# Retention: values centred per head in place of the outputs, no mean products, the variance a head sooner, decay powers ahead of the normalization

## The reference, cut to what matters

```python
def retention_branch(q, k, v, gate, log_decay, pad):
    ...
    q = rotate(q, pos, XPOS_THETA, RET_QK_DIM) * (RET_QK_DIM ** -0.5)
    k = rotate(k, pos, XPOS_THETA, RET_QK_DIM)
    ...
    o = retention_dir(qc, kc, vc, log_decay[0], True) + flip(
        retention_dir(flip(qc), flip(kc), flip(vc), log_decay[1], False))
    ...
    mu = jnp.mean(o, axis=-1, keepdims=True)
    var = jnp.mean(jnp.square(o - mu), axis=-1, keepdims=True)
    o = (o - mu) * lax.rsqrt(var + EPS)
    o = o.reshape(B, L, RET_V).astype(gate.dtype)
    return o * jax.nn.silu(gate)
```

## Time and profile before

| what | value |
|---|---|
| median of 3 runs | 4152.93 us (4151.59 to 4163.54) |
| profiled execution, span from first to last instruction | 4148.7 us |
| profiled execution's own time around it | not shown apart; the span is 4.2 us below the median |
| TensorE busy | 3974.4 us, 96% |
| VectorE, ScalarE, GpSimd busy | 54%, 35%, 21% |
| mean granted clock of TensorE | 0.975 of 2.4 GHz |

### The profile page before, as it was taken

How to read it: one execution, slowest core, us unless ns; L and a number is a source line. 1 busy time by engine, 2 the same in 40 slices (tenths; PEclk the granted TensorE clock), 3 DMA queues, 4 the chain that set the end, 5 groups by cost and what they waited for, 6 DMA issues and landing times. The chain is left out here.

```text
span 4148.7 us, 55847 instructions
## 1 busy us (share of the span) xinstructions
PE 3974.4 (96%) x22416; PEld 3453.2 (83%) x22416; DVE 2243.2 (54%) x3931; ACT 1471.3 (35%) x2120; POOL 860.5 (21%) x777
## 2 busy tenths in 40 slices
PE   8999999999899999999999999999999999999998
PEld 7877799999684568888777886789999998999997
DVE  4333446445434344645547544347997675666664
ACT  3144345222314433522237343333333333333332
POOL 1000013111200001312101520016756553111100
PEclk9998999999998999999989999999999999999999
DMA  3101123222110112322212022236756778888873
GB/s 132 52 31 41 46 82 112 92 87 96 57 62 27 45 46 92 119 91 102 81 61 77 31 67 66 87 98 202 227 186 194 247 251 272 286 265 265 265 245 122
DMA packets 232448, 519.43 MB, mean 125 GB/s; under 512 B 36160, under 2 KB 134592, under 8 KB 231808
## 3 DMA queue, kind: packets, MB, share of 16 engines
q1 hardware_dynamic: 160752, 400.75, 29.1%
q0 software_dynamic: 18432, 67.12, 4.6%
q10 hardware_dynamic: 53008, 47.99, 3.4%
HBM read 454.66 MB, written 60.82 MB: 124 GB/s over the span
## 5 line engine op out<-in xcount | busy, mean ns | idle before, releaser
L304 PE MATMUL PSM<-UX,PARTS 128*128 128x264 f32 (+3 forms) x3392 | 1192.3, 351 | 44.5 <-DVE UX L333 26.5
L305 PE MATMUL PSM<-UX,PARTS 128*128 128x264 f32 (+3 forms) x3392 | 1173.0, 346 | 0.0
L306 PE MATMUL PSM<-UX,PARTS 128*128 128x264 f32 (+3 forms) x3392 | 1169.8, 345 | 0.0
L272 DVE TENSOR_TENSOR PARTS<-RAW,PARTS 128x1024 fp32r<-128x1024 f32 x549 | 687.0, 1257 | 614.8 <-ACT PARTS L262 565.5
L262 ACT ACTIVATE PARTS<-RAW 128x1024 fp32r<-128x1024 f32 x612 | 644.8, 1056 | 993.7 <-PE PSM L306 493.3
L304 PEld LDWEIGHTS PSM<-UX,PARTS 128*128 128x128 f32 x3392 | 652.1, 192 | 134.5 <-DVE UX L333 37.0
L305 PEld LDWEIGHTS PSM<-UX,PARTS 128*128 128x128 f32 x3392 | 651.9, 192 | 60.3 <-issue 3.1
L306 PEld LDWEIGHTS PSM<-UX,PARTS 128*128 128x128 f32 x3392 | 651.4, 192 | 59.8
L2555 PE MATMUL PSM<-AC,PARTS 128*128 128x448 f32 x1024 | 374.7, 366 | 4.1 <-DVE AC L2802 4.1
L2557 PE MATMUL PSM<-AC,PARTS 128*128 128x448 f32 x1024 | 374.0, 365 | 0.0
L2556 PE MATMUL PSM<-AC,PARTS 128*128 128x448 f32 x1024 | 373.9, 365 | 0.0
(11 more groups left out here) (378 smaller groups left out, 5754.7 us busy)
## 6 DMA issues: line engine op xcount, KB each, us to landing
RAW<-w_ff_dram SPq DMA_DIRECT2D x128, 512.0 KB
RAW<-peer_u_dram SPq DMA_DIRECT2D x128, 512.0 KB
RAW<-peer_v_dram SPq DMA_DIRECT2D x128, 512.0 KB
RAW<-w_in_dram SPq DMA_DIRECT2D x116, 512.0 KB
acts_dram<-MQ ACTq DMA_DIRECT2D x128, 224.0 KB
MQ<-acts_dram SPq DMA_DIRECT2D x128, 224.0 KB
MQ<-gates_dram SPq DMA_DIRECT2D x128, 224.0 KB
RAW<-w_mix_o_dram SPq DMA_DIRECT2D x32, 512.0 KB
```

The lines of the kernel that those rows point to most:

```text
L272: e.tensor_tensor(p[:, 1024:2048], self.raw.of(i), p[:, 0:1024].bitcast(F), SUB).then_inc(V.sem, V.tick("w", i))
L304: e.matmul(dst, wh[k], xh_[k][:, lo:hi], start=(k == 0), stop=False, skip_group_check=True)
L305: e.matmul(dst, wh[k], xl_[k][:, lo:hi], start=False, stop=False, skip_group_check=True)
L306: m = e.matmul(dst, wl[k], xh_[k][:, lo:hi], start=False, stop=(k == kk - 1), skip_group_check=True)
```

## The change

- Each pair of heads' values is centred where it lies, over the 128 channels of each head, on VectorE right behind its copy out of PSUM (`centred_dve`): a sum and a subtraction for 16 rows and for 128 rows. The fourth group's centring stands behind the first head's decays.
- The mean product, its PSUM buffer and the subtraction out of PSUM are gone. ScalarE copies the sum and squares it, both straight from PSUM.
- The gate tile and the variance product of head h - 1 (before, h - 2) stand between scores and values of head h, so the stage has 9 rounds in place of 10.
- The decay powers of heads 0 and 1 are made in the projection stage; the exponential of the rates moves to its start.
- The scaling of head h - 2 on VectorE stands between the second and third score of head h.
- TensorE begins the scores when the last rotated tile is there (before, when VectorE had ended the projection stage).

```diff
@@ in_act @@
                 rstd_act(e, ("pre", l), TT, rsX, 1.0 / D, "ss", 7)
+                all_ = MH[:, oVec + 80:oVec + 112]
+                e.activation(all_, all_, ACT.Exp).then_inc(S.sem, S.tick("lg"))
...
             for t in range(5):
                 tok(t)
+                if t in (2, 3):
+                    decays_act(e, l, t - 2)
@@ in_dve @@
             for t in range(1, 5):
                 tok(t)
+                if t < 4:
+                    centred_dve(e, l, t)
+                if t < 3:
+                    logs_dve(e, l, t - 1)
...
+        def centred_dve(e, l, t):
+
+            c = 256 * (t - 1)
+            e.wait_ge(S.sem, S.at("tok", l, t, 3))
+            for (r, j0, j1), m in zip(((16, 0, 1), (128, 1, 5)), means[t - 1]):
+                x = vR[0:r, j0:j1, c:c + 256].rearrange("p j (a n) -> p j a n", a=2)
+                y = m[0:r].rearrange("p (j a) -> p j a", a=2)
+                e.wait_ge(V.sem, V.n)
+                e.tensor_reduce(y, x, AX.X, ADD).then_inc(V.sem, V.tick())
+                e.wait_ge(V.sem, V.n)
+                e.scalar_tensor_tensor(out=x, in0=y.unsqueeze(3).to_broadcast([r, j1 - j0, 2, 128]),
+                                       scalar=-1.0 / 128, in1=x, op0=MUL, op1=ADD).then_inc(
+                                           V.sem, V.tick("centred", l, t))
@@ ret_pe @@
-            e.wait_ge(V.sem, V.at("end", ("in", l)))
-            for h in range(10):
+            e.wait_ge(V.sem, V.at("rot", l, 12))
+            for h in range(9):
...
-                if h >= 2:
-                    i = first["fill", l] + h - 2
-                    tile_pe(e, ("g", l, h - 2), i, W.both(i), us(c0, n), n)
+                if h >= 1:
+                    i = first["fill", l] + h - 1
+                    tile_pe(e, ("g", l, h - 1), i, W.both(i), us(c0, n), n)
+                    b, back = ps.take("ss", ("ret", l, h - 1))
...
+                    e.wait_ge(S.sem, S.at("dev2", l, h - 1))
+                    gemm(e, b, [con["onesm"]], [sq2[(h - 1) % 2][:, 0:n]], n).then_inc(
+                        T.sem, T.tick("var", ("ret", l, h - 1)))
...
-                    gemm(e, b, [con["onesm"]], [sq2[h % 2][:, 0:n]], n).then_inc(T.sem, T.tick("var", ("ret", l, h - 2)))
-                if 1 <= h < 9:
-                    b, back = ps.take("mean", l, h - 1)
...
-                    gemm(e, b, [con["onesm"]], [oS[h - 1][:, 0:n]], n).then_inc(T.sem, T.tick("mean", l, h - 1))
@@ ret_act @@
+            for h in range(9):
+                if h >= 1:
+                    decays_act(e, l, h + 1)
+                    W.act(e, first["fill", l] + h - 1 + 3)
...
+                    rstd_act(e, ("ret", l, h - 1), n, sq2[(h - 1) % 2], 1.0, "var")
                 if h < 8:
                     e.wait_ge(T.sem, T.at("ret", l, h, 4))
                     e.activation(fv(oS[h][:, 0:n], n), pv(ps.of("ret", l, h), n), ACT.Copy).then_inc(
                         S.sem, S.tick("o", l, h))
+                    if h >= 2:
+                        e.wait_ge(V.sem, V.at("normed", l, h - 2))
+                    e.activation(fv(sq2[h % 2][:, 0:n], n), pv(ps.of("ret", l, h), n), ACT.Square).then_inc(
+                        S.sem, S.tick("dev2", l, h))
                     ps.give(S, "ret", l, h)
@@ ret_dve @@
-                if 1 <= h < 9:
-                    o = oS[h - 1]
-                    e.wait_ge(T.sem, T.at("mean", l, h - 1))
-                    e.scalar_tensor_tensor(out=fv(o[:, 0:n], n), in0=pv(ps.of("mean", l, h - 1), n), scalar=-1.0,
-                                           in1=fv(o[:, 0:n], n), op0=MUL, op1=ADD).then_inc(V.sem, V.tick("dev", l, h - 1))
-                    ps.give(V, "mean", l, h - 1)
+            for h in range(9):
                 if h < 8:
+                    decays(h, (0, 1))
+                if h >= 2:
+                    normed(h - 2)
+                if h < 8:
+                    decays(h, (2, 3, 4))
+                    if h >= 1:
+                        logs_dve(e, l, h + 1)
+                    else:
+                        centred_dve(e, l, 4)
+                if h >= 1:
+                    W.dve(e, first["fill", l] + h - 1 + 3)
+            normed(7)
```

More of the change, by code:

```diff
@@ L424, in program @@
         sq3, rsX = [wt(i) for i in range(3)], wt(3)
+        means = [(WK[:, 3 * TT + 16 * t:3 * TT + 16 * t + 2], WK[:, 3 * TT + 16 * t + 2:3 * TT + 16 * t + 10]) for t in range(4)]
         rx, ry, ut = [wt(4 + i) for i in range(3)], [wt(7 + i) for i in range(2)], [wt(9 + i) for i in range(3)]
@@ L578, in in_dve, with logs_dve, decays_act @@
             sin(12)
+            if l == 0:
+                e.wait_ge(S.sem, S.at("lg"))
+                for i in (0, 2):
+                    ap = MH[:, oVec + 80 + 8 * i:oVec + 88 + 8 * i]
+                    e.tensor_scalar(ap, ap, -1.0, None, MUL).then_inc(V.sem, V.tick())
             for t in range(1, 5):
                 tok(t)
+                if t < 4:
+                    centred_dve(e, l, t)
+                if t < 3:
+                    logs_dve(e, l, t - 1)
             stage_end(V, ("in", l))
+        def centred_dve(e, l, t):
[10 more added lines that the diff above has]
+                                           V.sem, V.tick("centred", l, t))
+        def logs_dve(e, l, h):
+            if h < 8:
+                dt = DT[h % 2]
+                e.wait_ge(V.sem, V.n)
+                e.tensor_scalar(dt, con["rel"], lg(l, 0, h), None, MUL).then_inc(V.sem, V.tick())
+                e.wait_ge(V.sem, V.n)
+                e.scalar_tensor_tensor(out=dt, in0=con["rel"], scalar=lg(l, 1, h), in1=dt, op0=MUL,
+                                       op1=MIN).then_inc(V.sem, V.tick("logs", l, h))
+        def decays_act(e, l, h):
+            if h < 8:
+                e.wait_ge(V.sem, V.at("logs", l, h))
+                e.activation(DT[h % 2], DT[h % 2], ACT.Exp).then_inc(S.sem, S.tick("decays", l, h))
         def in_pool(e, l):
@@ L645, in ret_act @@
             after_all(e, ("in", l))
[L646 to L661, removed]
+            for h in range(9):
+                if h >= 1:
+                    decays_act(e, l, h + 1)
+                    W.act(e, first["fill", l] + h - 1 + 3)
+                    e.wait_ge(T.sem, T.at("g", l, h - 1))
+                    if h >= 3:
+                        e.wait_ge(G.sem, G.at("gated", l, h - 3))
+                    e.activation(fv(gx[(h - 1) % 2][:, 0:n], n), pv(ps.of("g", l, h - 1), n), ACT.Silu).then_inc(
+                        S.sem, S.tick("g", l, h - 1))
+                    ps.give(S, "g", l, h - 1)
+                    rstd_act(e, ("ret", l, h - 1), n, sq2[(h - 1) % 2], 1.0, "var")
                 if h < 8:
@@ new lines, in decays @@
+            def decays(h, js):
+                dt = DT[h % 2]
+                for j in js:
+                    j0, nj = JT[j]
+                    e.wait_ge(T.sem, T.at("score", l, h, j))
+                    if j == 0:
+                        e.wait_ge(S.sem, S.at("decays", l, h))
+                    i = 5 * h + j
+                    if i >= 6:
+                        e.wait_ge(T.sem, T.at("ret", l, (i - 6) // 5, (i - 6) % 5))
+                    win = dt[0:nj, c0 - j0 + 400:c0 - j0 + 400 + n]
+                    e.scalar_tensor_tensor(out=fv(sd[i % 6][0:nj, 0:n], n), in0=pv(ps.of("score", l, h, j), n, nj),
+                                           scalar=0.125, in1=fv(win, n), op0=MUL, op1=MUL).then_inc(
+                                               V.sem, V.tick("decay", l, h, j))
+                    ps.give(V, "score", l, h, j)
```

59 lines of the change are left out of this document (7 added, 52 removed).

## The result

The changed kernel takes 4084.9 us (median of 4 runs, 4078.9 to 4090.1), the kernel before beside it 4152.3. The ratio is 0.9835, 95% interval 0.9815 to 0.9855. The profiled execution of the changed kernel took 4083.3 us, its span is 4081.5. The forecast was 4085. One execution of the experiment with waits of 1.23 us ran in a slow state (5623.5 us at a granted clock of 0.65) and is left out of that ratio.

The account below looks back on a forecast made before the run. TensorE's own sequence was taken to bound the kernel. Gains of 29.4 and 32.1 us in the stages and 2.6 and 4.1 in the tails sum to 68.2, giving 4085 us; own range 4078 to 4093, asked-for range 4076 to 4103.

Parts of the forecast that it names:

- Products: Retention stages: eight mean products in each layer leave TensorE, 8 x 0.97 + 8 x 0.94 = 15.3 us, all on the path.
- Waits and clock: Both retention stages: TensorE's waits go, 8.7 us in layer 0 and 9.1 in layer 1, and 28.5 us of clock return.
- the choice that the clock comes back: Retention stages: without waits the granted clock returns, worth 28.5 us, because the stretch 194 to 225 ran at 1.00.
- the closing waits: End of each retention stage: TensorE's wait for the squares, 0.52 us in layer 0 and 0.97 in layer 1, goes.
- (a): Rival, retention stages: the clock stays low because the half-array score mix makes the dips; 38.7 us won, 4114; chance 0.09.
- (d): Rival, retention stages: the denser sequence holds the clock down; at 60% half rate 31 us slower, 4184; chance 0.02.
- No new wait: Heads of the retention stages: PSUM buffers and squares are ready in time, so TensorE gets no new wait.
- 1.5 us and more to spare: Third and fourth scores of a head: the PSUM buffers they take are free at least this long before.
- Centring: VectorE in the projection: 3.4 us a group of two heads, hidden with 2.6 us cover; cost 0.
- Tails: Last gate product to first transposed attention product: 8.9 us in layer 0, 2.6 won; 10.9 in layer 1, 4.1 won.

## Why the prediction was right

*Products.* 15.3 us forecast. Put back alone they cost 13.8 to 16.6, and 13.9 by the heads of the trace. Shown, with a price per product some 0.1 us too high.

*Waits and clock.* 17.8 us of waits and 28.5 of clock, on the choice that the clock comes back. The split has a slip: the closing waits of 0.52 and 0.97 us lie behind the stages' ends at 339.9 and 1387.0. So the 61.5 us hold 16.3 of waits and some 30 of clock, and the sum is the same. The stages came out at 130.6 and 126.0 us where 130.7 and 126.2 were worked out, at a clock of 1.00. That the clock hung on the waits and not on the products is shown from both sides: taking only the waits out of the kernel before brought 33 to 37 us for 11.3 us of idle time, and putting ten waits of 1.23 us into the changed kernel took as much away. The rivals (a) and (d) are out. What decides whether a single wait brings a dip was not found. Of the two sections of the page "TensorE: Matmul & The Clock Gate" of the Trainium skill that the prediction weighs, "A second HAM failure mode: psum-queue depth-cycling", with its short idles between groups of products, fits these runs. The long waits for transfers of the other one, "HAM oscillation — how this bites in real kernels", were not needed: in the stages of the kernel before TensorE never waits for a transfer, its longest wait is 1.4 us, and the clock fell.

*No new wait.* ScalarE's order held: no head waits for the square or the logarithm. ScalarE in the changed kernel around the end of a head's values (222.66):

```profile
220.97 0.64 ACT L354 ACTIVATE WK<-WK 128x528 f32<-128x528 f32 x1
222.77 0.61 ACT L696 ACTIVATE WK<-PSM 128x528 f32<-128x528 f32 x1 [1.15 <-PE PSM L200]
223.28 0.60 ACT L700 ACTIVATE WK<-PSM 128x528 f32<-128x528 f32 x1
```

It is free 1.15 us before the copy can start, and the square ends at 223.9, 1.6 us ahead of the fourth score, which comes 2.9 us behind the values. How thin that is I had not said: with the variance product 4.8 us later it fails by 1.7 us a head, and costs all. The step "1.5 us and more to spare" was right because the variance moved ahead of the values, and the prediction should have named that as the condition.

*Centring.* Worked out at 3.4 us a group and a cover of 2.6 more; measured 3.3 and, with the centring doubled, 2.7. Cost 0, as forecast: left out altogether, it brings 2 us, which is within the spread of the runs.

*Tails.* Layer 0 forecast at 8.9 us, measured 9.1. Layer 1 forecast at 10.9 (of 9.6 to 12.0), measured 1332.98 - 1323.21 = 9.8, since its gate tile ran at full rate (5.75 us, the lower bound of the forecast's 5.8 to 8.2). From the stage's start to its first transposed attention product both layers won 32.0 and 37.6 us, 69.6 together; 67.2 reached the end, so that some 2 us were given back outside, nearly all behind layer 1. What took them was not tried.

*Luck.* The terms are shown to 1 or 2 us each. That their sum met the median to 0.1 us is luck: the tail of layer 1 won 1.2 us more than the sum has, the 2 us given back are not in it, and the four runs lie 11 us apart.

*What the parts are worth.* The waits in the scores, with their clock, 33 to 37 us; the mean products 14 to 17; the rest, 14 to 20, is the stages' starts and tails, of which the early decay powers are some 10 (7 by the profile up to the last stage, 14.9 by medians). These parts hold in this order of instructions only: a single misplaced variance outweighs them.

## What to carry to other kernels

Price a short wait of TensorE by the clock it costs too: look in the windows for a lower PEclk behind each, and take the whole interval from a stretch without a wait at full clock in place of summing idle times. Before removing work, look whether swapping two instructions on the engine that ends the wait removes it: here that alone brought about half the gain. When a product is moved, follow the in-order engine behind it to the buffer that it frees last.

## What the runs showed of the hardware

- Between score products (64 of the array's 128 rows) ten waits of 0.62 us cost 25.6 us, of 1.23 us 37.4, of 2.0 us 48.8. Waits of up to 0.5 us among the scores of the kernel before with its subtraction moved left the clock at 1.00. So did two waits of some 0.7 us in each layer among the full-array products of the projection. That the products around a wait make the difference is not shown: four waits are few, and three of the ten of 0.62 us brought no dip either.
- A wait of one length in one place does not always do the same: of five waits of 1.23 us in layer 0, three lengthened their head by 4.6 us, one by 3.0 and one by 1.5, the last with the clock at 1.00.
- A low clock can last without any wait to speak of: attention's narrow products (mostly 16 to 128 columns) without gate tiles ran at 0.53 for 29 us with TensorE busy 28.5 of them. The same kind of products without tiles ran at 1.00 for 17.4 us where they began at full clock and the longest wait was 0.3 us. Whether wider products would lift a clock that has fallen was not tried.
- A subtraction whose first operand is a mean broadcast over 128 elements (128 x 1024 in all) took VectorE 1.23 us, as much as the sum over the same elements (1.22) and less than the 1.30 us worked out from L692: the broadcast costs nothing that shows.
